# Stick-breaking heads over differences of the values, a new order of the chunks of one projection, and no filler products at the start of two attentions

## The reference

```python
def even_mixer(h, positions, w_in, q_a_norm, w_q_up, kv_a_norm, w_kv_up, q_norm, k_norm, w_o):
    cq, ckv, k_rope, sb_qkv = split_last(h @ w_in, [256, 128, 32, 3 * 512])
    q = (rms_norm_2(cq, q_a_norm) @ w_q_up).reshape(b, s, 8, 96)
    kv = (rms_norm_2(ckv, kv_a_norm) @ w_kv_up).reshape(b, s, 8, 64 + 64)
    k_nope, v = kv[..., :64], kv[..., 64:]
    k = concatenate([k_nope, k_rope for every head])
    q = rope_tail(rms_norm_2(q, q_norm)); k = rope_tail(rms_norm_2(k, k_norm))
    mla = causal_softmax_attention(q, k, v, 96 ** -0.5)
    sb = stick_breaking_attention(sq, sk, sv)      # sb_qkv in three
    return concatenate([mla, sb]) @ w_o

def stick_breaking_attention(q, k, v):             # mask: key before query
    z = q @ k.T * scale
    log_beta = log_sigmoid(z)
    log_1m_beta = where(mask, log_sigmoid(-z), 0.0)
    suffix = cumsum(log_1m_beta, reverse=True) - log_1m_beta
    a = where(mask, exp(log_beta + suffix), 0.0)
    return a @ v
```

## Time and profile before

| What | us |
|---|---|
| median of 3 runs (2159.96 to 2161.57) | 2160.92 |
| the profiled execution, its own time | 2163.58 |
| its span in the profile | 2161.7 |

### The profile page before, as it was taken

One profiled execution on the slowest core, in us unless ns is written; L12 is line 12 of the kernel. 1 busy time (PEld: TensorE's weight loads), 2 busy tenths in 40 slices (PEclk: granted clock), 3 DMA queues, 4 the chain that ended last, 5 costly groups with the idle time before them and its releaser, 6 DMA issues.

```text
span 2161.7 us, 29403 instructions
## 1 busy us (share of the span) xinstructions
PE 1979.8 (92%) x10416; PEld 1604.6 (74%) x10416; DVE 829.9 (38%) x1453; ACT 501.9 (23%) x1253; POOL 1116.5 (52%) x731
## 2 busy tenths in 40 slices
PE   5777899789999998987799999999999899999999
PEld 4666566578888887874478888887787578888887
DVE  4763667554535105545723222102453623212100
ACT  2111466322222102225511010101132511101100
POOL 4434001157666663622746666666553446666663
PEclk9887899699999998999899999999999999999999
DMA  4212000123333231312013333332321113333332
GB/s 135 59 57 88 0 0 4 37 88 98 97 97 115 89 102 56 89 34 69 11 50 98 97 97 96 94 95 76 83 85 59 41 40 92 97 96 95 97 97 88
DMA packets 125373, 161.99 MB, mean 75 GB/s; under 512 B 11670, under 2 KB 87398, under 8 KB 125286
## 3 DMA queue, kind: packets, MB, share of 16 engines
q1 hardware_dynamic: 121440, 159.97, 24.2%
q10 hardware_dynamic: 3846, 0.82, 0.2%
HBM read 158.66 MB, written 2.10 MB: 74 GB/s over the span
## 4 chain that ended last, share of the span: by engine, by line
PE 82%; DVE 9%; ACT 3%; issue 2%; POOL 2%; DMA 1%; ACTq 0%; SPq 0%; DVEq 0%; POOLq 0%
PE ps L718 22%; PE ps L720 22%; PE ps L719 22%; PE ps L1156 3%; PE ps L1085 2%; PE ps L1177 2%; PE ps L733 2%; PE ps L851 1%; PE ps L1168 1%; DVE tok L1827 1%; PE ps L1274 1%; PE ps L1126 1%; PE ps L1061 1%; DVE xt_lo L1837 1%; ACT dump L1395 1%
## 5 line engine op out<-in xcount | busy, mean ns | idle before, releaser
L447 POOL TENSOR_TENSOR w_lo<-raw,w_hi 128x1024 fp32r<-128x1024 f32 (+1 forms) x256 | 614.7, 2401 | 21.4
L445 POOL TENSOR_SCALAR w_hi<-raw 128x1024 fp32r<-128x1024 f32 (+1 forms) x256 | 275.4, 1076 | 574.0 <-PE ps L720 497.3
L718 PE MATMUL ps<-xt_hi,w_hi 128*128 128x512 f32 (+1 forms) x1160 | 432.9, 373 | 7.2 <-DVE xt_lo L1837 6.5
L720 PE MATMUL ps<-xt_hi,w_lo 128*128 128x512 f32 (+1 forms) x1160 | 432.2, 373 | 0.0
L719 PE MATMUL ps<-xt_lo,w_hi 128*128 128x512 f32 (+1 forms) x1160 | 432.2, 373 | 0.0
L718 PE MATMUL ps<-w_hi,xt_hi 128*128 128x512 f32 (+3 forms) x672 | 264.1, 393 | 28.7 <-ACT tok L1666 20.0
L720 PE MATMUL ps<-w_hi,xt_lo 128*128 128x512 f32 (+3 forms) x672 | 259.1, 386 | 0.0
L719 PE MATMUL ps<-w_lo,xt_hi 128*128 128x512 f32 (+3 forms) x672 | 258.9, 385 | 0.0
L718 PEld LDWEIGHTS ps<-xt_hi,w_hi 128*128 128x128 f32 x1160 | 219.2, 189 | 47.0 <-DVE xt_lo L1837 7.6
L720 PEld LDWEIGHTS ps<-xt_hi,w_lo 128*128 128x128 f32 x1160 | 219.0, 189 | 38.7
L719 PEld LDWEIGHTS ps<-xt_lo,w_hi 128*128 128x128 f32 x1160 | 219.2, 189 | 38.3
(11 more groups left out here) (317 smaller groups left out, 2480.3 us busy)
## 6 DMA issues: line engine op xcount, KB each, us to landing
raw<-in_w_up SPq DMA_DIRECT2D x88, 256.0 KB
raw<-in_l_w_gate SPq DMA_DIRECT2D x88, 256.0 KB
raw<-in_l_w_up SPq DMA_DIRECT2D x88, 256.0 KB
raw<-in_l_w_down SPq DMA_DIRECT2D x40, 512.0 KB
raw<-in_l_w_in SPq DMA_DIRECT2D x36, 512.0 KB
raw<-in_w_down SPq DMA_DIRECT2D x20, 512.0 KB
raw<-in_l_w_o SPq DMA_DIRECT2D x16, 512.0 KB
raw<-in_w_in SPq DMA_DIRECT2D x12, 512.0 KB
```

Source lines behind the costliest of these rows:

```text
L445: e.tensor_scalar(w_hi[:, s, 0:width], r, 1.0, 0.0, ALU.mult, ALU.add).then_inc(split, 1)
L447: e.tensor_tensor(w_lo[:, s, 0:width], r, w_hi[:, s, 0:width].bitcast(F32), ALU.subtract).then_inc(split, 1)
L718: e.matmul(o, s_hi, m_hi, start=start, stop=False)
L720: return e.matmul(o, s_lo, m_hi, start=False, stop=stop)
```

## The change

The chunks come in the order CQ, SQ, Q0, K0, SK, Q1, K1, SV. K0 and K1 get rows of their own (tok_k), their squares and later km_b lie in the gains. The turns of K0 and K1 stand behind the last slab of SK and SV. The first scores of mix wait for Q0 and K0 and three tiles of SV, round 1 for the rest. The stick heads' scan runs in place; TensorE turns c itself, ScalarE and VectorE write 1 - c when they copy the turned blocks, and the values are replaced by the differences v[j] - v[j-1]: SP copies v shifted by one row into v_back in three transfers, GpSimd clears the first row and subtracts in four instructions in rounds 6, 8, 10 and 12. GpSimd's 32 subtractions and VectorE's four memsets go, and stick steps are turned two rounds after their scores instead of three. One gain load waits for score 16. The filler products in pe_pair_attend go, in mix and in fox. The diff, cut to its core:

```diff
@@ -299,10 +296,10 @@
     IN1 = [(0, 512), (512, 512), (1024, 280), (1304, 512), (1816, 256)]
-    IN2 = [(416, 0, 4, 2), (512, 4, 4, 2), (384, 8, 1, 2), (512, 9, 4, 2), (384, 13, 1, 2), (512, 14, 1, 1),
-           (512, 15, 4, 2), (512, 19, 1, 1)]
-    CQ, SQ, Q0, SK, Q1, K0, SV, K1 = range(8)
-    HEAD_CHUNKS = {Q0: 0, Q1: 1, K0: 2, K1: 3}
+    IN2 = [(416, 0, 4, 2), (512, 4, 4, 2), (384, 8, 1, 2), (512, 9, 1, 1), (512, 10, 4, 2), (384, 14, 1, 2),
+           (512, 15, 1, 1), (512, 16, 4, 2)]
+    CQ, SQ, Q0, K0, SK, Q1, K1, SV = range(8)
+    HEAD_CHUNKS = {Q0: 0, K0: 1, Q1: 2, K1: 3}
...
@@ -411,15 +408,19 @@
         qw, kw, iw = A["l0_mla_w_q_up_2"], A["l0_mla_w_kv_up_2"], A["l0_w_in_2"]
-        slabs = (two_kt(iw, 0, 416) + two_kt(iw, 416, W) + [[(0, cols(qw, 0, 384, slice(0, 2)))]] + two_kt(iw, 928, W)
-                 + [[(0, cols(qw, 384, 384, slice(0, 2)))], [(0, cols(kw, 0, W, slice(0, 1)))]]
-                 + two_kt(iw, 1440, W) + [[(0, cols(kw, W, W, slice(0, 1)))]])
+        slabs = (two_kt(iw, 0, 416) + two_kt(iw, 416, W)
+                 + [[(0, cols(qw, 0, 384, slice(0, 2)))], [(0, cols(kw, 0, W, slice(0, 1)))]] + two_kt(iw, 928, W)
+                 + [[(0, cols(qw, 384, 384, slice(0, 2)))], [(0, cols(kw, W, W, slice(0, 1)))]] + two_kt(iw, 1440, W))
             sp_group(e, ph["in2"].g0 + i, slabs[4 * i:4 * i + 4])
-        gain_load(e, 6, at("in2_tp", 27))
+        e.wait_ge(*at("in2_copy", 32))
+        for a, b in ((1, 113), (113, P)):
+            e.dma_start(v_back[a:b, :, :], v2[a - 1:b - 1, :, W:D]).then_inc(sem("v_back"), 16)
+        e.dma_start(v_back[0:1, 1:NT, :], v2[P - 1:P, 0:NT - 1, W:D]).then_inc(sem("v_back"), 16)
+        sp_group(e, ph["out2"].g0, two_kt(A["l0_w_o_2"], 0, W))
+        gain_load(e, 6, at("mix_s", 16))
         gain_load(e, 7)
-        with e.Fori(0, 2) as c:
-            sp_group(e, c + ph["out2"].g0, two_kt(A["l0_w_o_2"], c * W, W))
+        sp_group(e, ph["out2"].g0 + 1, two_kt(A["l0_w_o_2"], W, W))
...
@@ -508,13 +509,13 @@
         def turn_round(self, g):
-            return g + (2 if self.is_soft(g) else 3)
+            return g + 2
         def turned_in(self, r):
-            return [g for g in (r - 2, r - 3) if 0 <= g < self.steps and self.turn_round(g) == r]
+            return [r - 2] if 2 <= r < self.steps + 2 else []
         def values_round(self, p):
-            return 4 * p + (9 if p < self.soft else 10)
+            return 4 * p + 9
...
@@ -551,26 +545,17 @@
                 sem(f"{name}_lo"), 1)
-        def sticks(g):
-            for x in range(2):
-                u = 2 * (g - 4 * st.soft) + x + 1
-                e.wait_ge(*at(f"{name}_sc", u))
-                r = run_at(g, x)
-                n = (4 - g % 4) * P
-                e.tensor_tensor(prob_at(g, x), r[:, 1:n + 1], r[:, 0:n], ALU.subtract).then_inc(sem(f"{name}_w"), 1)
                 split_slab(e, *slabs[r], SLAB)
+            if steps and r in steps:
+                value_step(steps[r])
                     halves(p)
-            if st.is_soft(r - 1) or r - 1 >= st.steps:
-                continue
-            sticks(r - 1)
...
@@ -635,7 +620,16 @@
                 split_cols(e, ph["in2"].g0 + i // 4, i % 4, k, n)
-        pool_pairs(e, mix, {3 + 4 * s: (ph["out2"].g0, s) for s in range(4)})
+        e.wait_ge(*at("in2_copy", 32))
+        e.memset(v_back[0:1, 0, :], 0.0).then_inc(sem("v_first"), 1)
+        def value_step(t):
+            if t == 0:
+                e.wait_ge(*at("v_first", 1))
+                e.wait_ge(*at("v_back", 48))
+            e.tensor_tensor(v2[:, t, W:D], v2[:, t, W:D], v_back[:, t, :], ALU.subtract).then_inc(sem("v_step"), 1)
+        pool_pairs(e, mix, {3 + 4 * s: (ph["out2"].g0, s) for s in range(4)}, {6: 0, 8: 1, 10: 2, 12: 3}, value_step)
...
@@ -685,11 +679,11 @@
         mla_heads(qm, 0, 0),
+        mla_heads(km_a, 0, 1),
         mla_heads(qm, 4, 0),
-        mla_heads(km_a, 0, 1),
+        mla_heads(km_b, 0, 1),
         [],
-        mla_heads(km_b, 0, 1),
...
@@ -1047,7 +1041,7 @@
             else:
-                e.wait_ge(*at(f"{name}_w", 2 * (g - 4 * st.soft) + 2))
+                e.wait_ge(*at(f"{name}_sc", 2 * (g - 4 * st.soft) + 2))
...
@@ -1080,6 +1074,8 @@
                 e.wait_ge(*output_free(st, p - 1))
+            if p == st.soft:
+                e.wait_ge(*at("v_step", NT))
...
@@ -1090,13 +1086,14 @@
         for r in st.rounds:
+            if r == 1:
+                for s, v in later:
+                    e.wait_ge(s, v)
                     e.wait_ge(s, v)
-                for _ in range(FILL):
-                    e.matmul(bank(6), ident_b[:, :], dump[:, 0:W], start=True, stop=True)
...
@@ -1301,12 +1298,14 @@
         pe_project(e, "in2", [(*chunk, x2.get(c, x_model)) for c, chunk in enumerate(IN2)], t_plan(T_IN2),
-                   {(SQ, 2): (CQ,), (Q0, 0): (SQ,), (SK, 2): (Q0,), (Q1, 0): (SK,), (SV, 1): (Q1,), (SV, 3): (K0,)},
+                   {(SQ, 2): (CQ,), (Q0, 0): (SQ,), (SK, 2): (Q0,), (SK, 3): (K0,), (Q1, 0): (SK,), (SV, 2): (Q1,),
+                    (SV, 3): (K1,)},
         heads_of = lambda v: lambda p, x, kb: v[:, kb, (2 * p + x) * HD:(2 * p + x + 1) * HD]
-        pe_pair_attend(e, mix, mix_scores, heads_of(v2), [at("in2_tpa", 12), at("in2_tpd", 15), at("in2_copy", 32)], [])
+        pe_pair_attend(e, mix, mix_scores, heads_of(v2), [at("in2_tpa", 6), at("in2_tpd", 9), at("in2_copy", 31)], [],
+                       [at("in2_copy", 32), at("in2_tpa", 12), at("in2_tpd", 15)])
...
@@ -1469,14 +1468,24 @@
                     e.activation(dst, src, ACT.Copy, scale=scale).then_inc(*od.done(*at(f"{name}_tpa", count)))
+    def squares_at(name, nth, t):
+        return k_squares[:, t, :] if name == "in2" and nth % 2 else scratch[:, t % 2, :]
+    def squares_free(name, nth, t):
+        if name == "in2" and (nth % 2 or t < 2):
+            return 4 * (nth - 1) if nth >= 2 else 0
+        return max(0, 4 * nth + t - 1)
         i = 4 * nth + t
-        if i >= 2:
-            e.wait_ge(*at(f"{name}_red", i - 1))
+        if squares_free(name, nth, t):
+            e.wait_ge(*at(f"{name}_red", squares_free(name, nth, t)))
         n = rows.shape[1] * (rows.shape[2] if len(rows.shape) == 3 else 1)
-        s = scratch[:, t % 2, 0:n]
+        s = squares_at(name, nth, t)[:, 0:n]
...
@@ -1603,8 +1612,11 @@
                     e.wait_ge(*at(f"{name}_t", g + 1))
-                    e.activation(turned_probs(st, g, y), turned_bank(g, y), ACT.Copy).then_inc(
-                        *od.done(*is_turned(st, g, y)))
+                    if st.is_soft(g):
+                        op = e.activation(turned_probs(st, g, y), turned_bank(g, y), ACT.Copy)
+                    else:
+                        op = e.activation(turned_probs(st, g, y), turned_bank(g, y), ACT.Identity, scale=-1.0, bias=1.0)
+                    op.then_inc(*od.done(*is_turned(st, g, y)))
...
@@ -1616,6 +1628,8 @@
             e.wait_ge(*at(f"{name}_o", p + 1))
+            if p == st.soft:
+                e.wait_ge(*at(f"{name}_lo", st.soft))
...
@@ -1739,14 +1753,16 @@
                     act_head_squares(e, od, "in2", HEAD_CHUNKS[c], t, staged("in2", c)[:, t, 0:384])
+                    if t == 1:
+                        act_rstd(e, od, "in2", HEAD_CHUNKS[c] + 1, 16)
         for c in range(8):
-            act_copies(e, od, "in2", c, ends[c], copy2(c), plan, c not in (K0, SV))
-            if c == CQ or c in HEAD_CHUNKS:
+            act_copies(e, od, "in2", c, ends[c], copy2(c), plan, c not in (K0, K1, SV))
+            if c in (CQ, K0, K1):
                 act_rstd(e, od, "in2", 1 if c == CQ else HEAD_CHUNKS[c] + 2, 8 if c == CQ else 16)
-            for x in {Q1: (), K0: (Q1, K0), SV: ()}.get(c, (c,)):
+            for x in {Q0: (), K0: (Q0, K0), Q1: (), K1: (Q1,), SV: (K1,)}.get(c, (c,)):
...
@@ -2050,10 +2066,8 @@
                 e.wait_ge(*at(f"{name}_p", 2 * g + x + 1))
-                if h >= 4:
-                    e.wait_ge(*at(f"{name}_w", 2 * (h - 4) + x + 1))
-                e.tensor_tensor_scan(run_at(g, x)[:, 0:n][:, ::-1], prob_at(g, x)[:, ::-1],
-                                     one[:, 0:1].broadcast_to([P, n]), 1.0, ALU.mult, ALU.mult).then_inc(
+                keep = prob_at(g, x)[:, ::-1]
+                e.tensor_tensor_scan(keep, keep, one[:, 0:1].broadcast_to([P, n]), 1.0, ALU.mult, ALU.mult).then_inc(
...
@@ -2067,7 +2081,11 @@
                     e.wait_ge(*at(f"{name}_t", g + 1))
-                    e.tensor_copy(turned_probs(st, g, y), turned_bank(g, y)).then_inc(*od.done(*is_turned(st, g, y)))
+                    if st.is_soft(g):
+                        op = e.tensor_copy(turned_probs(st, g, y), turned_bank(g, y))
+                    else:
+                        op = e.tensor_scalar(turned_probs(st, g, y), turned_bank(g, y), -1.0, 1.0, ALU.mult, ALU.add)
+                    op.then_inc(*od.done(*is_turned(st, g, y)))
...
@@ -2298,14 +2311,14 @@
             nth = HEAD_CHUNKS[c]
```

(4 more changed lines are left out.)

40 lines of the change are left out of this document (14 added, 26 removed).

## The result

| | before | after |
|---|---|---|
| median, us (lowest to highest) | 2161.24 (2159.96 to 2161.57) | 2131.97 (2128.06 to 2132.83) |
| ratio to before, 95% interval | | 0.9862 [0.9845, 0.9879] |
| profiled execution, own time / span | 2163.58 / 2161.7 | 2128.06 / 2126.3 |
| mean granted clock | 0.959 | 0.965 |

29.3 us less. The forecast was 2128.6, in a range from 2121 to 2141. Two more measurements of the same changed kernel gave medians of 2130.94 and 2130.09.

A forecast was written before the change was run, and what follows sets the result against it. TensorE, 92% busy, was taken as the bound, with time to win only in its idle time or low clock. Gains 21.0 + 1.3 + 10.0 = 32.3 us took the median 2160.92 to 2128.6, range 2121 to 2141.

The forecast's parts named there:

- 4.1 of new idle: In in2, new TensorE waits: K0's pacing 0.9, the chunk after each K 2 x 1.15, Q1 0.85 us.
- The low clock: In in2, time lost at the slow clock: 1.7 us in the last turn and 4.0 in slow matmuls.
- The slack of the norms: In in2, K1's norms and rotations would be ready before TensorE asks, with about 2 us to spare.
- rival B: In in2, K's norms are late or the low clock returns: 15 of 21 come, 2134.6 us; chance 0.12.
- The same holds for K0: In in2, K0's norms behind SK would also fit, as K1's do with about 2 us to spare.
- The overlap argument: At mix's start, scores 2 needs bank 0, free at 998.3; fillers hold it until 999.3, so 0.8 to 0.9 gained.
- the round trip: In the stick half, transposes, two ScalarE copies, next transposes: waits of 0.8 to 0.9, some six times, 4.8 us.
- The longer copies: In the stick half, new constants might lengthen ScalarE's copies (0.69 against 0.60 for 512), costing 0.8 us.
- rival D: Shifted rows of v crawl over one engine, out2's first slab lands 50 us after mix starts; 2162 to 2166, chance 0.03.
- A: Stick half: TensorE's pauses keep the low clock for most value groups, only 5 of 10 come; 2133.6 us, chance 0.14.
- C: Nothing new bites in any part: gains 23 + 1.5 + 12.2, giving 2124 us; chance 0.10.
- E: Stick half: Identity with scale and bias needs another table than sigmoid, 41 us of loads on ScalarE; 2155, chance 0.03.

The follow-up runs named there:

- squares_shared: Changed kernel with the squares of K0 and K1 sharing the two scratch rows with those of Q0 and Q1 again; 2149.85 us, in2 90.19.
- fillers_back: Changed kernel with the eight filler products back in round 1 of mix and of fox; 2133.58 us.
- before_again: The kernel before, unedited, measured and profiled a second time; 2160.78 us.
- after_again: The changed kernel, unedited, measured and profiled a second time beside the kernel before; 2130.94 us.
- one_transfer: Changed kernel with the shifted rows of v sent in one transfer of 127 partitions instead of two of 112 and 15; 2163.31 us.
- copies_first: Changed kernel with VectorE copying the turned softmax blocks before its stick scans in the two rounds that begin the stick half; 2127.32 us.
- the failure in the tail: copies_first plus VectorE taking one of the two copies of each turned block in the last three stick steps; 2128.36 us, stick half 49.33.

## Why the prediction was right

**Order of chunks: 21.0 expected, 22.4 measured.** The terms that left did so: 11.7, 5.9, 0.9 and 0.9, as the earlier trace rows listed them. Of the 4.1 of new idle only 1.9 came: Q1's wait is 0.9 (0.85 expected), but the chunk behind each K waits 0.5 once instead of 0.7 and 0.45, and K0 isn't paced by Q0's copies beyond the wait of 0.7 that was there before. The low clock gave back 5.0 where 5.7 was expected (1.7 for the turn and 4.0). Against the second profile of before the part is worth 21.4. The slack of the norms was judged wrongly both ways. By VectorE's timeline K1's last rotation ends at 961.92 and TensorE asks at 967.27, a slack of 5.3 where the working had 2. K0's last rotation:

```profile
928.55 0.29 DVE L1934 TENSOR_TENSOR tok_k<-tok_k,rot 128x128 f32<-128x128 f32 x1
```

It ends at 928.84, and TensorE asks at 929.12: 0.3. "The same holds for K0" was the loose step; it held by 0.3 us. What used the slack up is what rival B had named, VectorE's operations stretching while GpSimd splits a slab. One of K0's rotations took 2.46 where the others take 0.29 (2.45 and 2.46 in the other two profiles of the changed kernel):

```profile
923.48 2.46 DVE L1934 TENSOR_TENSOR tok_k<-tok_k,rot 128x128 f32<-128x128 f32 x1
923.39 2.41 POOL L462 TENSOR_TENSOR w_lo<-raw,w_hi 128x1024 fp32r<-128x1024 f32 x1
```

One more such stretch would have left TensorE waiting. That this forecast came out was in this place luck.

**What the working didn't see** is that the two edits of this part multiply. It credited the rows for the squares with one wait and the low clock; squares_shared shows 90.2 - 70.6 = 19.6 lost without them. The forecast for both together didn't suffer, since it walked through the combined order.

**Fillers: 0.8 and 0.5 expected, 0.8 and 0.45 measured**, and 0.7 and 0.4 by fillers_back. The overlap argument (scores 2 wants the bank only at the end of the first exponential) holds: TensorE now waits 0.7 for it, the fourth wait of the first fence of waits, where it used to be busy with fillers.

**Stick half: 10.0 expected, 8.6 measured.** The second part was to take 38.5 and took 39.9, with 31.1 of work (31.4 expected, the slow group in the tail included) and 8.8 of idle (6.3). The mechanism was right, and the term that was mis-sized is the round trip of transposes and ScalarE's copies: 4.8 for "some six times in all", where it comes nine times, 7.1 in all (the six waits of 4.3 that name ScalarE, and the three of 0.93 that name a scan but end with a copy). The low half: 1.5 as said. VectorE's scans cost TensorE nothing, as the working had it. The longer copies (0.8) didn't come: 0.607 against 0.595. The stretch ahead stayed as it was, 10.82 against 10.86, with its wait of 3.63.

**Transfers.** Hidden, as the share of 0.98 shows. What decided it was the split in two pieces: one_transfer turned the gain into nothing, at 2163.31, inside the 2162 to 2166 of rival D. Its chain was right too, GpSimd at the slab with the inverses behind it; its rate was not, 24 to 27 GB/s instead of 18, so the slab came 45 us after the start of mix and not 50. The Trainium skill, "DMA: Bandwidth & Descriptors", section on why a DMA increments its semaphore by 16, says that a transfer goes over the largest number of engines up to 16 that divides its partitions, with 127 giving one; one_transfer agrees, at a share of 0.06 to 0.07. The same page's table at its head gives about 27 GiB/s, 29 GB/s, for one engine; the 24 to 27 GB/s here are a little under it.

**Rivals.** A (the low clock stays for most value groups): of the five groups that it counted one was slow in after, 3.84, against three before, so it didn't come; the group ahead of them, behind the stop of 3.6 us, was slow in both (3.57, and 3.8 before). B came near only in K0's norms. C, nothing new bites: no, the idle time left in the second part is 8.8. D's chain is the one that one_transfer shows. E: ScalarE loads a table once at the start of the stick half and once behind it, 1.28 us each on its timeline, and none between, with identity copies all along; so here the trace agrees with the Trainium skill, "ScalarE: Activation LUTs", that identity is in every set.

**The sum.** 32.3 against 32.2 between the two first profiles, and the medians moved by 29.3. The forecast of 2128.6 was 3.4 too low. Of this, 1.0 is the low clock in in2 that only the first profile of before has. That the parts add up to 32.3 is in part luck: in2 came 1.4 above its term with that profile, the stick half 1.4 below. The rest isn't in the touched stretches, and the profiled executions weren't typical: that of before stood 2.3 above its median, that of after 3.9 below. The untouched stretches scatter by about what is missing (the first takes 901.1 and 901.8 before, 898.4 to 900.2 after; the last 489.9 and 492.5 before, 491.4 after). The second pair of profiles, before_again and after_again, differs by 30.5 where the touched stretches differ by 31.2. I can't tell from profiles of single executions whether the changed kernel's medians carry more low clock; that stays open.

## What to carry to other kernels

When two small edits remove waits on the same chain, cost them together and apart: here the order alone was worth 2.9 us and the buffers alone 7.9, and both 22.5. When an engine falls below its bound, write out its order inside one period, since what stands directly ahead of the instruction that others want counts, not the sum (it explains the gain of copies_first and the failure in the tail). Where a wait covers several semaphores, hold the name that the view gives against the code: three waits "for a scan" were waits for ScalarE's copies, and would have sent the next change to the wrong engine. Look at the partition count of every transfer between partitions: 112 and 15 cost nothing, 127 cost 33 us. Compare kernels by stretches between instructions that both have; these repeated within 0.11 us in three profiles of the changed kernel, and within 1.0 in two of the kernel before, where the totals of the changed kernel scattered by 9; and part each stretch into idle and busy time, since the granted clock can move the second with every wait the same.
